# A mixture-of-experts stage: each expert's rows gathered behind its predecessor's down products, and a fifth block of expert 0 loaded ahead

## The chip, the cores and the metric

One Trainium2 chip, one of its cores. The metric is device time in microseconds (us) of one execution. The kernel before has a median of 1833.7 us over 3 runs (1831.3 to 1837.27).

## The reference, cut to what matters

The program computes three blocks of a network one after the other (256 tokens, 1024 channels, all in f32). The change lies in the second half of the first block, an expert-choice layer of 16 experts, each of which takes the 32 tokens that rate it highest:

```python
def _expert_choice_ffn(h, w_router, b_router, w_gate, w_up, w_down):
    b, n, d = h.shape
    cap = max(1, EC_CAPACITY_FACTOR * n // N_EXPERTS)          # 2 * 256 // 16 = 32
    logits = h.astype(jnp.float32) @ w_router.astype(jnp.float32) + b_router.astype(jnp.float32)
    aff = jax.nn.softmax(logits, axis=-1)
    gate, idx = lax.top_k(jnp.swapaxes(aff, 1, 2), cap)
    xs = jax.vmap(lambda hb, ib: hb[ib])(h, idx)
    a = jnp.einsum('becd,edf->becf', xs, w_gate)               # w_gate, w_up: 16 x 1024 x 2048
    u = jnp.einsum('becd,edf->becf', xs, w_up)
    y = jnp.einsum('becf,efd->becd', jax.nn.silu(a) * u, w_down) * gate[..., None].astype(h.dtype)
    return jax.vmap(lambda yb, ib: jnp.zeros((n, d), yb.dtype).at[ib.reshape(-1)].add(yb.reshape(-1, d)))(y, idx)
```

The weights of one expert are 3 matrices of 1024 x 2048 f32 (25.2 MB together), of all sixteen 402.7 MB. The rest of the program (a mixer before, two more blocks behind) is not touched.

## The kernel before, in words

All weights come through a **ring** of 4 slots in SBUF. A slot holds one block of 2 MB (128 partitions x 4096 f32). SyncE (SP) issues the loads in program order, all on one queue; before the load of a block it waits until TensorE has used the block four places earlier (semaphore `ring_used`, one step for each block used up). The layers ahead of the experts use 21 blocks (`EXP_BLOCK0`), then come the experts, then `dense2`.

An expert has 12 blocks: 0 to 3 gate, 4 to 7 up, 8 to 11 down. For a gate or up block TensorE runs 32 matmuls (stationary: 32 columns of `XSE`, the expert's 32 rows turned so that channels lie on partitions; moving: 512 columns of the weights), into bank 0 for gate and bank 1 for up. ScalarE takes silu of bank 0, VectorE multiplies with bank 1 (`HID`), TensorE turns it, ScalarE copies it out (`HIDT`), and then come the products with the down blocks into banks 2 and 3 (in the code `c` = 0 to 3 is down block 8 + c). ScalarE and VectorE each copy one of these banks to `YE`. Last, eight matmuls (`SELT`, a 32 x 256 matrix that places the rows at their tokens and weights them; in the trace they are line L2077, "the combine" below) add the expert's rows to banks 4 to 7, where the sum over all experts grows. Only then do the gate products of the next expert start, on `XSE` of that expert. Experts 1 to 14 are one loop body on every engine; 0 and 15 are written out.

**Where the rows come from.** A gather is a matmul with a matrix of zeros and ones, `SEL` (token x slot, 16 x 32 slots): for each of 8 channel tiles 4 matmuls (2 halves of the tokens, times a high and a low part of the values, `HT_HIGH` and `HT`). For expert 0 this is done first, with 32 columns of `SEL`, 32 matmuls in all (the function `gather`), and VectorE writes `XSE` from the banks with scale and shift (L2675). For the other 15 experts it is done once, behind the down products of expert 0: `gather_rest` runs 32 matmuls with 480 columns each, into banks 0 and 1 in turn; ScalarE (`tokens_in`) writes each of the 8 results with scale and shift into a table `XS` (17 tiles of SBUF, 1 KB a partition each); and VectorE copies 256 columns of it to `XSE` for each next expert (`next_rows`, L2695).

**Blocks loaded ahead.** Of expert 0 the blocks in `EXTRA` (2, 4, 5 and 6) don't go through the ring, but into SBUF that is free at that time (`AHEAD`: two halves of 1 MB each). SP issues them behind the first four blocks of expert 0 that do use the ring (0, 1, 3 and 7), in front of the remaining ones, and TensorE waits for them by `extra_in`. The next ring block of expert 0, block 8, is loaded in two halves: the first when the first half of block 0's slot has been read (`half_read`), the second when all of it has.

```python
            in_ring = [b for b in range(EXP_BLOCKS) if b not in EXTRA]
            for b in in_ring[:RING]:
                load(first_expert_block(b), expert_source(0, b).unsqueeze(1))
            sp.wait_ge(s.ring_used, EXP_BLOCK0)
            for b, halves in zip(EXTRA, AHEAD):
                ...
                    sp.dma_start(halves[kk], ...).then_inc(s.extra_in, 16)
            for b in in_ring[RING:]:
                ...
```

Line numbers of the trace: L1516, L1559 and L1561 are ring loads of SP outside loops, L1554 the loads ahead, L1570 the loop of experts 1 to 15, L1575 `dense2`; L1644 is the helper behind most matmuls, L2057 the turning of `HID`, L2077 the combine, L2121 the helper behind all of ScalarE's activations, L2705 VectorE's copy to `YE`, L2702 `SELT`.

## Time and profile before

| | before |
|---|---|
| median of 3 runs | 1833.7 us (1831.3 to 1837.27) |
| the profiled execution | 1832.58 us |
| its span | 1830.8 us |
| busy: TensorE / its weight loads | 1462.0 us (80%) / 990.6 us (54%) |
| busy: VectorE, ScalarE, GpSimd | 710.5 us (39%), 589.2 us (32%), 35.6 us (2%) |
| moved by DMA | 573.55 MB, mean 313 GB/s |
| mean granted TensorE clock | 0.897 |

The span begins with the first instruction and ends with the last; 1.8 us of the execution lie outside it. The page shows the span in 40 slices of 45.8 us, each with the busy tenths of the engines, the granted clock and what the DMA engines moved. The experts' products stand from 230 us to 1145 us, slices 6 to 25. In the chain of waits a step is either an engine's work or "DMA x<-y", time in which the end of a transfer was waited for.

### The profile page before, as it was taken

What the parts mean: (1) busy time and instruction counts of PE and PEld (TensorE: products, weight loads), DVE (VectorE), ACT (ScalarE), POOL (GpSimd) and SP (SyncE); (2) the same over time, 40 slices, a digit from 0 to 9 for tenths busy, and PEclk for the clock granted to TensorE, in tenths of its full rate; (3) what the DMA queues carried; (4) which work ended last, traced back from release to release, by engine and by line L of the source; (5) the groups of instructions that cost most, each with busy time, mean ns of one, the idle gap of its engine ahead of it and who ended that gap; (6) DMA issues with size and microseconds to landing.
All of it is one profiled execution on the core that took longest, in us unless ns stands there. A gap on an engine that the chain in (4) does not pass through costs nothing.

```text
span 1830.8 us, 25067 instructions
## 1 busy us (share of the span) xinstructions
PE 1462.0 (80%) x10432; PEld 990.6 (54%) x10432; DVE 710.5 (39%) x1256; ACT 589.2 (32%) x1007; POOL 35.6 (2%) x40
## 2 busy tenths in 40 slices
PE   6999996665656666666656667999999999999998
PEld 4787941211112111112111112998998999999997
DVE  4457610000000000000000000897995999478764
ACT  6444510000000000000000001677475776465654
POOL 0000200000000000000000000000000000000101
PEclk9999897888887787877878877999999999999999
DMA  9566799999999999999999999657453755554330
GB/s 399 221 246 235 301 386 424 428 428 429 429 429 428 428 429 428 429 428 428 428 429 429 429 428 427 242 188 207 154 185 132 267 206 190 191 173 173 139 139 24
DMA packets 53266, 573.55 MB, mean 313 GB/s; under 512 B 4928, under 2 KB 15424, under 8 KB 16576
## 3 DMA queue, kind: packets, MB, share of 16 engines
q1 hardware_dynamic: 47440, 563.10, 75.7%
q10 hardware_dynamic: 5744, 9.28, 1.4%
q8 instruction: 61, 1.00, 0.2%
q14 instruction: 21, 0.17, 0.0%
HBM read 568.04 MB, written 4.33 MB: 313 GB/s over the span
## 4 chain that ended last, share of the span: by engine, by line
DMA 43%; PE 37%; DVE 16%; ACT 2%; issue 1%; SPq 0%; DVEq 0%; ACTq 0%
PE bank L1644 36%; DMA ring<-in_w_up 14%; DMA ring<-in_w_down 14%; DMA ring<-in_w_gate 13%; DVE ring_rounded L2437 6%; DVE work L929 2%; DVE work L747 1%; DMA ring<-in_dense 1%; DVE work L919 1%; DVE work_rounded L2360 1%; DMA work<-decay_rows 1%; ACT work L2121 1%; DVE work L738 1%; ACT weights_high_rounded L2121 1%; DMA ring<-in_w_ada 1%
## 5 line engine op out<-in xcount | busy, mean ns | idle before, releaser
L1644 PE MATMUL bank<-ring,work 128*32 128x512 f32 x3008 | 483.9, 778 | 293.5 <-DMA ring<-in_w_up 126.3
L1644 PEld LDWEIGHTS bank<-ring,work 128*32 128x32 f32 x3008 | 94.1, 127 | 646.8 <-DMA ring<-in_w_up 206.6
L2121 ACT ACTIVATE work<-bank 128x512 f32<-128x512 f32 (+3 forms) x152 | 72.8, 492 | 998.6 <-PE bank L1644 667.9
L2437 DVE TENSOR_TENSOR ring_rounded<-ring,weights_high_rounded 128x1024 fp32r<-128x1024 f32 x208 | 252.6, 1219 | 80.9 <-ACT weights_high_rounded L2121 80.9
L2121 ACT ACTIVATE weights_high_rounded<-ring 128x1024 fp32r<-128x1024 f32 x244 | 254.0, 1051 | 42.7 <-PE bank L1644 41.4
L2691 DVE TENSOR_TENSOR work<-work,bank 128x512 f32<-128x512 f32 x16 | 16.5, 1030 | 582.7 <-PE bank L1644 582.7
L1644 PE MATMUL bank<-h_high_rounded,weights_high_rounded 128*128 128x256 f32 x1264 | 185.5, 286 | 1.7 <-ACT h_high_rounded L2121 1.5
L1644 PE MATMUL bank<-h_high_rounded,ring_rounded 128*128 128x256 f32 x1264 | 174.5, 277 | 2.4 <-DVE ring_rounded L2448 2.4
L1644 PE MATMUL bank<-h_normed_rounded,weights_high_rounded 128*128 128x256 f32 x1264 | 173.7, 278 | 0.0
L1644 PEld LDWEIGHTS bank<-h_high_rounded,weights_high_rounded 128*128 128x128 f32 x1264 | 161.3, 188 | 13.2 <-issue 6.9
L1644 PEld LDWEIGHTS bank<-h_high_rounded,ring_rounded 128*128 128x128 f32 x1264 | 158.3, 188 | 2.9 <-DVE ring_rounded L2448 2.8
L1644 PEld LDWEIGHTS bank<-h_normed_rounded,weights_high_rounded 128*128 128x128 f32 x1264 | 157.9, 188 | 0.2
L1644 PE MATMUL bank<-work_rounded,weights_high_rounded 128*128 128x256 f32 x1152 | 152.1, 283 | 5.3 <-ACT work_rounded L2121 5.3
L1644 PEld LDWEIGHTS bank<-work_rounded,weights_high_rounded 128*128 128x128 f32 x1152 | 141.9, 192 | 9.4 <-ACT work_rounded L2121 6.9
L2705 DVE COPY work<-bank 128x512 f32<-128x512 f32 x16 | 11.1, 692 | 284.0 <-PE bank L1644 284.0
L2077 PE MATMUL bank<-work 128*128 128x256 f32 x256 | 70.1, 434 | 13.5 <-DVE work L2705 13.5
L2077 PEld LDWEIGHTS bank<-work 128*128 128x128 f32 x256 | 55.0, 221 | 44.2 <-issue 35.1
L1644 PE MATMUL bank<-work_rounded,ring_rounded 128*128 128x256 f32 x544 | 74.5, 280 | 0.0
L1644 PEld LDWEIGHTS bank<-work_rounded,ring_rounded 128*128 128x128 f32 x544 | 68.3, 191 | 0.0
L1627 POOL TENSOR_TENSOR squares<-squares 128x256 f32<-128x256 f32 x30 | 30.1, 1005 | 1770.8 <-ACT squares L2121 1770.8
L2448 DVE TENSOR_TENSOR ring_rounded<-ring,weights_high_rounded 128x1024 fp32r<-128x1024 f32 x36 | 43.6, 1221 | 44.1 <-ACT weights_high_rounded L2121 43.8
L2121 ACT ACTIVATE work<-work,params 128x256 f32<-128x256 f32 x85 | 48.5, 581 | 27.3 <-DVE work L738 17.8
(269 smaller groups left out, 1206.4 us busy)
## 6 DMA issues: line engine op xcount, KB each, us to landing
ring<-in_w_gate SPq DMA_DIRECT2D x63, 2048.0 KB, 16.2
ring<-in_w_down SPq DMA_DIRECT2D x63, 2048.0 KB, 16.2
ring<-in_w_up SPq DMA_DIRECT2D x61, 2048.0 KB, 16.3
ring<-in_dense SPq DMA_DIRECT2D x60, 2048.0 KB, 8.4
ring<-in_w_ada SPq DMA_DIRECT2D x12, 2048.0 KB, 13.5
work<-in_w_up SPq DMA_DIRECT2D x3, 1024.0 KB, 14.6
bias_diagonals<-work SPq DMA_DIRECT2D x2, 1536.0 KB, 14.9
ring<-in_dense SPq DMA_DIRECT2D x2, 1024.0 KB, 18.7
```

Of the source, the lines that this page charges most:

```text
L738: v.tensor_tensor(dst, B[(PU2 + u) % 4][:, 0:SEQ], RS[:, 1, :], ALU.mult).then_inc(s.dense_sb, 1)
L747: v.scalar_tensor_tensor(out=o[:, shift:SEQ], in0=SCALED2[:, u % 4, 0:SEQ - shift], scalar=w[:, 3 - shift:4 - shift], in1=o[:, shift:SEQ], ...
L919: v.tensor_tensor(SCALED[:, u % 4, :], B[(PU2 + L_UP + u) % 4][:, 0:SEQ], RS[:, 1, :], ALU.mult).then_inc(s.dense_sb, 1)
L929: v.scalar_tensor_tensor(out=o[:, shift:SEQ], in0=SCALED[:, u % 4, 0:SEQ - shift], scalar=ffn_weight(u, 2 - shift), in1=o[:, shift:SEQ], o ...
L1627: nc.gpsimd.tensor_tensor(SQ[:, 0, :], SQ[:, 0, :], SQ[:, k, :], ALU.add).then_inc(s.squares_added, 1)
L1644: return nc.tensor.matmul(o, lhsT, rhs, start=start, stop=stop)
L2077: last = nc.tensor.matmul(B[4 + k // 2][:, (k % 2) * SEQ:(k % 2 + 1) * SEQ], YE[:, k * P:(k + 1) * P], SELT[:], start=False, stop=final an ...
L2121: return nc.scalar.activation(o, i, f, **kw)
L2360: v.tensor_tensor(as_r(full), full, as_r(high) if high.dtype == F32 else high, ALU.subtract).then_inc(s.act_low, 1)
L2437: v.tensor_tensor(as_r(w), w, w_high[:, buffer, :], ALU.subtract).then_inc(s.w_low, 1)
L2448: v.tensor_tensor(as_r(w), w, w_high[:, unit % HIGHS, :], ALU.subtract).then_inc(s.w_low, 1)
L2691: v.tensor_tensor(HID.rearrange("p (i q) -> p q i", i=4), rows_apart(SG), rows_apart(B[1][:]), ALU.mult).then_inc(s.hid_ready, 1)
```

## The change

- `EXTRA` has a fifth block, 8 (the first down block of expert 0), and `AHEAD` a fifth place, tiles 8 to 23 of the work area, which held part of the table `XS`. TensorE waits for it by a semaphore of its own, `down_in`. Block 9 is now the one loaded in two halves. All later blocks stand one place earlier in the ring (`EXP_BASE` is 16, was 17).
- `XS`, `gather_rest`, ScalarE's `tokens_in`, VectorE's `next_rows` and a memset of 0.27 us are gone.
- Behind the down products of each expert but the last, and in front of its combine, TensorE runs `gather_next(e)`: 32 matmuls with 32 columns of `SEL` each, all into bank 1, which are picked by a register in the loop. VectorE, behind its copy to `YE`, waits for them and writes `XSE` in 8 operations out of bank 1, as it does for expert 0.

```diff
-EXTRA = (2, 4, 5, 6)
+EXTRA = (2, 4, 5, 6, 8)
 EXP_BASE = EXP_BLOCK0 - len(EXTRA)
...
-        XS = tiles(8, 17).rearrange("p (k j) -> p k j", k=KT)
...
-                 (h_high, tiles(29, 8)), (squares, h_normed))
+                 (h_high, tiles(29, 8)), (squares, h_normed), (tiles(8, 8), tiles(16, 8)))
...
-                    sp.dma_start(halves[kk], expert_source(0, b)[:, kk * DEXP:(kk + 1) * DEXP]).then_inc(s.extra_in, 16)
+                    sp.dma_start(halves[kk], expert_source(0, b)[:, kk * DEXP:(kk + 1) * DEXP]).then_inc(
+                        s.extra_in if b < 8 else s.down_in, 16)
...
-            def gather_rest():
-
-                pe.wait_ge(s.sel_ready, 2)
+            def gather_next(e):
+
                 for k in range(KT):
-                    if k >= 2:
-                        pe.wait_ge(s.xs_sb, k - 1)
-                    gather(k, B[k % 2][:, CAP:], slice(CAP, EXPERTS * CAP))
-                pe.wait_ge(s.slots_ready, 1)
-                clear(2)
-                clear(3)
+                    for part in (HT_HIGH, HT):
+                        for t in range(TT):
+                            last = mm(B[1][:, k * CAP:(k + 1) * CAP], as_r(part[:, t, k * P:(k + 1) * P]),
+                                      as_r(SEL[:, t, bass.ds(e * CAP + CAP, CAP)]), part is HT_HIGH and t == 0,
+                                      part is HT and t == TT - 1)
+                last.then_inc(s.xs_mm, 1)
...
-                    last.then_inc(s.ring_used, 1)
+                    if not (first and 8 + c in EXTRA):
+                        last.then_inc(s.ring_used, 1)
 
                 if first:
-                    gather_rest()
+                    pe.wait_ge(s.sel_ready, 2)
+                if not final:
+                    gather_next(e)
+                if first:
+                    pe.wait_ge(s.slots_ready, 1)
+                    clear(2)
+                    clear(3)
                 pe.wait_ge(s.selt_ready, e + 1)
...
-            def tokens_in():
-
-                for k in range(KT):
-                    act.wait_ge(s.xs_mm, KT + k + 1)
-                    fn(XS[:, k, CAP:EXPERTS * CAP], B[k % 2][:, CAP:], ACT.Identity, scale=ROW_SCALE[:, k:k + 1],
-                       bias=ROW_SHIFT[:, k:k + 1]).then_inc(s.xs_sb, 1)
...
-            v.memset(XS[:, :, EXPERTS * CAP:], 0.0)
...
-                def next_rows():
-                    v.tensor_copy(XSE, XS[:, :, bass.ds(e * CAP + CAP, CAP)]).then_inc(s.xse_ready, 1)
-
                 if first:
                     other_slots()
-                else:
-                    next_rows()
...
                 v.tensor_copy(YE[:, 512:1024], B[3][:]).then_inc(s.y_high, 1)
-                if first:
-                    dve.wait_ge(s.xs_sb, KT)
-                    next_rows()
+                if final:
+                    return
+                dve.wait_ge(s.xs_mm, e + (KT + 1))
+                for k in range(KT):
+                    last = v.tensor_scalar(XSE[:, k, :], B[1][:, k * CAP:(k + 1) * CAP], ROW_SCALE[:, k:k + 1],
+                                           ROW_SHIFT[:, k:k + 1], ALU.mult, ALU.add)
+                last.then_inc(s.xse_ready, 1)
```

How the instructions stand now. First SP, before and with the change, from the last loads ahead to the loop of the experts (`squares`, `h_normed` and `work` are places of loads ahead; `in_w_down` is the source of blocks 8 to 11). Before:

```order
L1554 DMA squares<-in_w_up 128x2048
L1554 DMA h_normed<-in_w_up 128x2048
L1559 DMA ring<-in_w_down 128x2048
L1561 DMA ring<-in_w_down 128x2048
L1516 DMA ring<-in_w_down 128x4096 x3
```

With the change:

```order
L1553 DMA squares<-in_w_up 128x2048
L1553 DMA h_normed<-in_w_up 128x2048
L1553 DMA work<-in_w_down 128x2048 x2
L1559 DMA ring<-in_w_down 128x2048
L1561 DMA ring<-in_w_down 128x2048
L1515 DMA ring<-in_w_down 128x4096 x2
```

Two loads of 1 MB, block 8, stand in front of the load that waits for `half_read`; three ring blocks follow (9 in halves, 10, 11) where there were four.

Second TensorE in the loop of experts 1 to 14, from the turning of `HID` (L2057, now L2059) to the end of the body. Before:

```order
L2057 MATMUL bank<-consts,work 128x128 x4
L1644 MATMUL bank<-ring,work 32x512 x24
L2034 REGISTER_ALU
L1644 MATMUL bank<-ring,work 32x512 x8
L2077 MATMUL bank<-work 128x256 x8
L2085 REGISTER_ALU
L2085 COMPARE_AND_BRANCH
```

With the change:

```order
L2059 MATMUL bank<-consts,work 128x128 x4
L2036 REGISTER_ALU
L1644 MATMUL bank<-ring,work 32x512 x32
L1644 ISA
L1644 MATMUL bank<-work_rounded 128x32
L1644 ISA
L1644 MATMUL bank<-work_rounded 128x32 x31
L2086 MATMUL bank<-work 128x256 x8
L2094 REGISTER_ALU
L2094 COMPARE_AND_BRANCH
```

The 32 small matmuls of the gather, with two register instructions, stand between the down products and the combine.

Third VectorE in the same loop. Before:

```order
L2691 TENSOR_TENSOR work<-work,bank 128x128x4
L2695 ISA
L2695 COPY work<-work 128x256
L2702 ISA
L2702 TENSOR_SCALAR work<-consts,small 128x256
L2704 REGISTER_ALU
L2705 COPY work<-bank 128x512
```

With the change:

```order
L2690 TENSOR_TENSOR work<-work,bank 128x128x4
L2695 ISA
L2695 TENSOR_SCALAR work<-consts,small 128x256
L2697 REGISTER_ALU
L2698 COPY work<-bank 128x512
L2701 REGISTER_ALU
L2703 TENSOR_SCALAR work<-bank,small 128x32 x8
```

The copy to `XSE` in the middle of the body is gone, and 8 operations that read bank 1 stand at its end.

## Rows read from the trace of the kernel before

**Rows 1.** The page: DMA's rate in 40 slices; chain of waits by engine

```profile
GB/s 399 221 246 235 301 386 424 428 428 429 429 429 428 428 429 428 429 428 428 428 429 429 429 428 427 242 188 207 154 185 132 267 206 190 191 173 173 139 139 24
...
DMA 43%; PE 37%; DVE 16%; ACT 2%; issue 1%; SPq 0%; DVEq 0%; ACTq 0%
```

**Rows 2.** Windows: us; busy PE, PEld, DVE, ACT, POOL (count); clock, DMA share, GB/s

```profile
205.00:230.50 25.50, 23.02 (x150) 21.88 (x153) 18.75 (x72) 12.01 (x33) 5.24 (x6) 0.78 1.00 410
230.50:236.00 5.50, 5.50 (x44) 1.38 (x40) 0.00 (x0) 0.00 (x0) 0.00 (x0) 0.78 0.52 161
236.00:253.00 17.00, 16.31 (x125) 5.04 (x117) 2.71 (x5) 1.20 (x2) 0.00 (x0) 0.91 1.01 422
253.00:256.00 3.00, 3.00 (x32) 0.99 (x28) 0.00 (x0) 0.00 (x0) 0.00 (x0) 0.94 0.94 360
256.00:273.00 17.00, 17.00 (x88) 10.04 (x84) 0.99 (x2) 6.62 (x9) 0.00 (x0) 1.00 1.00 427
273.00:277.00 4.00, 4.00 (x40) 1.15 (x36) 0.00 (x0) 0.00 (x0) 0.00 (x0) 1.00 0.93 340
...
282.00:1120.00 838.00, 520.55 (x3028) 141.24 (x3024) 30.24 (x56) 25.08 (x42) 0.00 (x0) 0.80 1.01 429
```

**Rows 3.** Timeline, loads issued by SP around the end of the loads ahead

```profile
214.15 0.43 SPq L1554 DMA_DIRECT2D h_normed<-in_w_up  x1
232.27 0.33 SPq L1559 DMA_DIRECT2D ring<-in_w_down  x1
233.54 0.33 SPq L1561 DMA_DIRECT2D ring<-in_w_down  x1
...
252.61 0.35 SPq L1570 DMA_DIRECT2D ring<-in_w_gate  x1
254.86 3.77 SPq L1570 DMA_DIRECT2D ring<-in_w_gate  x3
273.47 3.77 SPq L1570 DMA_DIRECT2D ring<-in_w_up  x3
```

**Rows 4.** Timeline, TensorE from expert 0's down products to expert 1's gate products

```profile
249.33 8.77 PE L1644 MATMUL bank<-ring,work 128*32 128x512 f32 x64 [0.69 <-ACT work L2121]
...
258.03 7.97 PE L1644 MATMUL bank<-work_rounded 128*128 128x480 f32 x32
...
271.49 7.07 PE L1644 MATMUL bank<-ring,work 128*32 128x512 f32 x64
```

**Rows 5.** Timeline and lines: expert 0's gather, VectorE's eight operations, a register-picked operation

```profile
225.83 3.90 PE L1644 MATMUL bank<-work_rounded 128*128 128x32 f32 x32
...
L2675 DVE TENSOR_SCALAR work<-bank,small x8: 309/310/311, 226.7 to 229.8; 128x32 f32<-128x32 f32 x8
...
L2702 DVE TENSOR_SCALAR work<-consts,small x16: 395/400/412, 247.9 to 1122.0; 128x256 f32<-128x256 f32 x16
```

**Rows 6.** Timeline, two of the passages between experts 1 to 15; last row a full-clock combine

```profile
555.68 6.10 PE L2077 MATMUL bank<-work 128*128 128x256 f32 x16 [0.90 <-DVE work L2705]
563.70 11.02 SPq L1570 DMA_DIRECT2D ring<-in_w_up  x4
575.61 1.92 PE L1644 MATMUL bank<-ring,work 128*32 128x512 f32 x16 [1.27 <-DMA ring<-in_w_up]
...
383.35 13.47 SPq L1570 DMA_DIRECT2D ring<-in_w_up  x4
399.40 2.98 PE L1644 MATMUL bank<-ring,work 128*32 128x512 f32 x16 [2.97 <-DMA ring<-in_w_up]
...
612.70 3.69 PE L2077 MATMUL bank<-work 128*128 128x256 f32 x16 [0.90 <-DVE work L2705]
```

**Rows 7.** Windows: the products of one block at each level of the clock

```profile
551.20:554.70 3.50, 3.50 (x16) 0.53 (x16) 0.00 (x0) 0.00 (x0) 0.00 (x0) 0.50 1.01 431
381.36:384.70 3.34, 1.93 (x17) 0.42 (x16) 0.00 (x0) 0.00 (x0) 0.00 (x0) 1.00 1.04 442
```

**Rows 8.** Timeline, the last down products of expert 15

```profile
1138.43 1.92 PE L1644 MATMUL bank<-ring,work 128*32 128x512 f32 x16 [0.99 <-DMA ring<-in_w_down]
```

More of the change, by code:

```diff
@@ L103 @@
 state_mm score_mm sd_ready y_mm mod_ready start_in toep_mm toep_sb rot_mm state_sb qfb_ready y_sb y_sums
-ysq_ready turn_ready router_mm aff_ready aff_tr topk_ready slot_mm sel_ready xs_sb xs_mm slots_ready
-half_read xse_ready hid_ready hid_tr hidt_sb selt_ready y_low y_high acc_done act_step params_in ctx_in x_in
+ysq_ready turn_ready router_mm aff_ready aff_tr topk_ready slot_mm sel_ready xs_mm slots_ready
+half_read down_in xse_ready hid_ready hid_tr hidt_sb selt_ready y_low y_high acc_done act_step params_in ctx_in x_in
 toep_stored ramp_ready xi_ready g_silu yc_ready yvar_ready yrstd_ready token_squares expert_in
@@ L2025, in expert_block @@
                         if b in EXTRA:
-                            pe.wait_ge(s.extra_in, 32 * len(EXTRA))
+                            if b < 8:
+                                pe.wait_ge(s.extra_in, 32 * sum(extra < 8 for extra in EXTRA))
+                            else:
+                                pe.wait_ge(s.down_in, 32)
                             return AHEAD[EXTRA.index(b)]
                         blk = first_expert_block(b)
-                        if b == 8:
+                        if b == 9:
                             pe.wait_ge(s.first_units, 32)
@@ L2300, in _, with expert @@
             fn(small(120, 2 * KT), B[6][:, CAP:CAP + 2 * KT], ACT.Copy).then_inc(s.ht_sb, 1)
-            def tokens_in():
-                for k in range(KT):
-                    act.wait_ge(s.xs_mm, KT + k + 1)
-                    fn(XS[:, k, CAP:EXPERTS * CAP], B[k % 2][:, CAP:], ACT.Identity, scale=ROW_SCALE[:, k:k + 1],
-                       bias=ROW_SHIFT[:, k:k + 1]).then_inc(s.xs_sb, 1)
-            def expert(e, gates, first=False):
+            def expert(e, gates):
                 act.wait_ge(s.ring_used, e * EXP_BLOCKS + gates)
@@ L2315, in expert @@
                 fn(YE[:, 0:512], B[2][:], ACT.Copy).then_inc(s.y_low, 1)
-                if first:
-                    tokens_in()
-            expert(0, first_expert_block(3) + 1, first=True)
+            expert(0, first_expert_block(3) + 1)
             with act.Fori(1, EXPERTS) as e:
@@ L2685, in other_slots, with expert @@
                 dve.wait_ge(s.slots_ready, 1)
-            def expert(e, first=False):
-                dve.wait_ge(s.ring_used, e * EXP_BLOCKS + (EXP_BASE + 8))
+            def expert(e, products, first=False, final=False):
+                dve.wait_ge(s.ring_used, e * EXP_BLOCKS + products)
                 dve.wait_ge(s.silu_sb, e + 1)
@@ L2705, in expert @@
                 v.tensor_copy(YE[:, 512:1024], B[3][:]).then_inc(s.y_high, 1)
-                if first:
-                    dve.wait_ge(s.xs_sb, KT)
-                    next_rows()
-            expert(0, first=True)
-            with dve.Fori(1, EXPERTS) as e:
-                expert(e)
+                if final:
[5 more added lines that the diff above has]
+                last.then_inc(s.xse_ready, 1)
+            expert(0, first_expert_block(7) + 1, first=True)
+            with dve.Fori(1, EXPERTS - 1) as e:
+                expert(e, EXP_BASE + 8)
+            expert(EXPERTS - 1, EXP_BASE + 8, final=True)
             for q in range(2):
```

## The prediction

> **What bounds the kernel now.** I read the slices of the page first. From the seventh to the twenty-fifth the DMA engines move 424 to 429 GB/s without a let-up; behind that it is 242 and less, but for one slice of 267 [rows 1]. So the experts' stage runs at the pace of the weight stream, whatever TensorE does in its gaps; 43% of the chain of waits is DMA [rows 1]. The windows say it closer: 429 GB/s over 838 us without a break [rows 2]. At that rate a block of 2,097,152 bytes takes 4.89 us. The last down product of expert 15 still waits for its block [rows 8], so whatever the stream gains or loses before 1138 us, the end gains or loses. Nothing behind that point is touched.
>
> The question is therefore: where does the stream lose time, and what does the change do there? The windows answer with length x (1 - rate / 429) [rows 2]:
> - 230.5 to 236 us: 5.5 x (1 - 161/429) = 3.44 us. The loads ahead, the last of them issued at 214.15 us, have all landed. The next load waits for the first half of block 0 to be read and goes out at 232.27, its second half at 233.54 [rows 3].
> - 236 to 253: 17 x 7/429 = 0.28 us.
> - 253 to 256: 3 x 69/429 = 0.48 us.
> - 256 to 273: 0.08 us.
> - 273 to 277: 4 x 89/429 = 0.83 us.
>
> Together 5.1 us. From 282 us on there is nothing to win.
>
> **The price of a late issue.** Both small losses are loads issued too shortly before the queue ran out. Behind 230.5 us four blocks (8 to 11 of expert 0) were moved: 230.5 + 4 x 4.89 + 3.44 + 0.28 = 253.8 us. The next load was issued at 252.61 [rows 3], 1.2 us ahead, and 0.48 us were lost. Four blocks on it is 253.8 + 0.48 + 19.56 + 0.08 = 273.9; the issue at 273.47 is 0.4 us ahead, and 0.83 us were lost. So a load must be issued some 1.5 us before the queue is empty (1.2 + 0.48 = 1.7 and 0.4 + 0.83 = 1.2), and each us less costs about one.
>
> **The change, part by part.**
>
> *The fifth block ahead.* Its two loads stand behind the one of 214.15 us and in front of the wait for half of block 0, with no wait of their own. They are issued by 215.5 us while the queue is full to 230.5. The stream goes on to 235.4, and block 9 comes at 232.27, 3 us ahead. The loss of 3.44 us is gone: **-3.44**. Nothing ahead of it in the queue is delayed, and SP has nothing to issue between 214.6 and 232.3. On the ring the load of expert 1's block 0 now follows the up products of block 7. Its block 1 follows block 9's down product, as before: 254.86 us [rows 3].
>
> *The next two edges.* The queue now holds blocks 8 to 11 and expert 1's block 0: 230.5 + 5 x 4.89 + 0.28 = 255.2 us. The issue at 254.86 is 0.4 us ahead, which by the same pair costs 0.83 us (it was 0.48). Then 255.2 + 0.83 + 3 x 4.89 + 0.08 = 270.8 us. Block 4 of expert 1 needs block 0 used. TensorE ends the down products at 258.03 and then ran 32 gather matmuls of 480 columns in 7.97 us [rows 4]. With 32 columns the same count took 3.90 us [rows 5]. Clears and combine follow, 266.0 to 271.49, 5.5 us, and block 0's products, 1.98 us up to the issue at 273.47 [rows 3, 4]: 258.03 + 3.90 + 5.5 + 1.98 = 269.4, 1.4 us ahead. I charge 0.48 for it, the nearer of the two prices (it was 0.83). Together 1.31 against 1.31: **0**. Eight activations of ScalarE and the memset leave too; the activations went with the matmuls that are gone, the memset lay beside products.
>
> *The 14 other passages.* Each gets 32 matmuls of 32 columns on TensorE in front of the combine: 3.90 us. TensorE stood idle 0.9 us there anyway for the copies to `YE` [rows 6], so the gate products come 3.0 us later. VectorE's eight operations take 8 x 0.31 = 2.5 us [rows 5] and run beside the combine of 3.69 us [rows 6]; they end about a us before it. The one thing queued behind is the next load. How late may it be? In the tightest of the 14 passages the load of block 4 was issued at 563.70 and used at 575.61 [rows 6]: 11.9 less 4.89 for itself and 1.5 for the lead leaves **5.5 us** of slack. In the loosest, 383.35 to 399.40 [rows 6], it is 9.7, and the mean of the 14 is 7.8. The delay of 3.0 fits in all: **0** in the time, some 55 us more TensorE work. If the cover went, each passage would cost up to 3 us. Unknown is what a register in the operand costs a matmul. On VectorE the nearest case costs nothing: `SELT` takes 395 to 412 ns, once written out and 15 times with a register [rows 5]. I take 0. The upper end is the 480-column matmul, 249 ns each, so 8.0 us a gather and a delay of 7.1. That loses 1.6 us in each of the two tightest passages and about 1.7 in the three next, 5 us in all.
>
> **Sum:** 1832.58 (the profiled execution, 1830.8 of it span) - 3.44 = 1829.1 us. The median of the runs lies 1.1 us above that execution, so I forecast **1830.3 us**, 0.19% less.
>
> The lead is where a page and the rows differ. The Trainium skill, DMA: Bandwidth & Descriptors, section Anatomy of one DMA, gives a transfer a fixed cost of about 2.0 us. If all of it had to be in front, as an estimate the two edges would lose 1.6 and 0.6 us, and the time would be 0.9 us higher than mine. The rows show 1.2 and 1.7, and I go by them.
>
> **The rivals.**
> - *The gap only moves.* The stream is half a us short at 255 us already. If the products of blocks 8 and 9 both run at half clock (a block takes 3.5 us at 0.50 and 1.93 at 1.00 [rows 7]), they end at 256.3, 1.1 us behind the empty queue, and the loss there is 2.6 us, 1.8 more than I charge. A slow gather, combine and gate product could cost another 1 to 2 us at 271. That gives all 3.4 back: about 1834 us. For it: the clock is 0.78 and 0.91 in the windows before [rows 2]. Against it: four down blocks took 8.77 us in this trace [rows 4], one slow block and three fast. Chance 0.12.
> - *Every gather at half clock.* The mean clock of the stage is 0.80 [rows 2]. A gather then takes 3.90 x 3.5/1.93 = 7.1 us, the delay is 6.2, and only the three passages with slack of 5.5, 5.5 and 6.05 lose, 1.6 us together: 1832 us. Against it: 9 of 14 combines ran in 3.69 us, at full clock, and the gather adds work there. Chance 0.08. The Trainium skill, TensorE: Matmul & The Clock Gate, section HAM oscillation, describes just such short bursts between DMA waits as falling back to 1.2 GHz; by that page this case would be the normal one; here the blocks' products ran at both levels [rows 7], and most combines at the upper one.
> - *Slower: the passages become the bound.* If a gather with register operands takes 9 us (280 ns a matmul, more than twice the row), gate products come 8.1 us late, over the mean slack of 7.8. The fourteen lose about 10 us together: 1830.3 + 10 = 1840 us. At 10 us it would be 20. Below about 7 us nothing happens, and a net loss begins at 8 us. For it: no row shows TensorE with such an operand. Against: VectorE's. Chance 0.09.
> - *The change doesn't do what it says.* The fifth block could be held until the gap is over; its loads have no wait and stand first in line, so only something unseen in the queue could. 1833.7 us, chance 0.03.
>
> **How the numbers follow.** The forecast has 0.68. A measurement of this kernel can tell about 0.3% (5.5 us) from no change. Even all 5.1 us regained would be 0.28%, so "faster" needs the scatter of the runs, which is -2.4 to +3.6 us about the median: 0.15. "Slower" is the third rival and a little of the first: 0.11. The rest, 0.74, is "same". The range: below, the 4.7 us that could be regained at best (all but the 0.36 lost at running pace) and most of the scatter, 1826.5; above, the first two rivals with scatter, 1837. The third rival and the far tails stay out.
>
> **What would show it.** Right: the window from 230.5 to 236 at 429 GB/s; one small dip at 254 to 257 us and at most one at 270 to 272; from there 429 GB/s to the end; the last product of expert 15 at about 1135.0 instead of 1138.43; 32 matmuls of 122 ns between down products and combine, and the combine 3 us later against its last down product. Wrong: dips in the rate between 300 and 1120 us (third rival, or the second if the clock is at 0.50 where they stand), a gap of over 2 us near 255 or 271 (the first), or no idle gap gone at 231 (the fourth).

## The result, and the profile after

The changed kernel takes 1836.9 us (median of 22 runs, 1830.9 to 1843.7) against 1833.7 (22 runs of the kernel before beside them): a ratio of 1.0019, 95% interval 1.001 to 1.0028. It is slower by about the amount that I had forecast as a gain; the interval lies just above 1. The profiled execution took 1835.9 us, 1834.1 of it span, 3.3 more than before, at a mean granted clock of 0.887 (0.897 before).

The page of the changed kernel: busy time of the engines, DMA's rate in 40 slices, the chain of waits by engine, and the combine's group.

```profile
PE 1526.5 (83%) x10880; PEld 1072.1 (58%) x10880; DVE 734.7 (40%) x1359; ACT 583.3 (32%) x999; POOL 35.6 (2%) x40
...
GB/s 400 223 243 239 301 383 426 414 428 429 428 428 428 423 430 428 429 428 424 430 428 429 428 425 424 252 187 197 150 192 138 261 204 193 193 173 172 139 138 24
...
PE 40%; DMA 39%; DVE 16%; ACT 3%; issue 1%; SPq 0%; DVEq 0%; ACTq 0%
...
L2086 PE MATMUL bank<-work 128*128 128x256 f32 x256 | 92.7, 541 | 0.9 <-DVE work L2698 0.9
```

TensorE is busy for 65 us more (1462.0 before). The combine, whose code did not change, went from 70.1 to 92.7 us: 22.6 of the 65. In the chain TensorE has taken 3 to 4% from DMA.

The stream first. Windows of the changed kernel, columns as in [rows 2]:

```profile
230.50:236.00 5.50, 5.50 (x28) 1.28 (x32) 0.00 (x0) 0.00 (x0) 0.00 (x0) 0.53 1.01 420
236.00:253.00 17.00, 16.31 (x125) 5.34 (x121) 2.70 (x5) 1.19 (x2) 0.00 (x0) 0.89 1.02 432
253.00:256.00 3.00, 3.00 (x20) 0.79 (x16) 0.00 (x0) 0.00 (x0) 0.00 (x0) 0.50 0.68 284
256.00:269.00 13.00, 13.00 (x87) 7.60 (x80) 2.53 (x9) 0.60 (x1) 0.00 (x0) 0.89 0.83 337
273.00:277.00 4.00, 4.00 (x44) 1.21 (x40) 0.00 (x0) 0.00 (x0) 0.00 (x0) 1.00 0.77 283
282.00:1120.00 838.00, 582.95 (x3460) 221.84 (x3452) 53.19 (x154) 25.08 (x42) 0.00 (x0) 0.78 1.00 427
```

The gap at 231 is closed: 420 GB/s where [rows 2] have 161. But 253 to 256 went from 360 to 284, behind it stands 337 for 13 us where 427 stood, and 273 to 277 went from 340 to 283. From 282 us on the rate is 427 instead of 429. Added up over windows of one us, as us x (1 - rate / 429):

| stretch, us | 230 to 245 | 245 to 262 | 262 to 282 | 282 to 1138 |
|---|---|---|---|---|
| before | 3.8 | 0.5 | 0.8 | 1.1 |
| after | 0.1 | 3.9 | 1.3 | 4.2 |

The 1.1 of the last column is what rounding of the rates leaves where nothing is lost; kernels below that lose nothing there have 0.8 to 1.3. Up to 282 us the changed kernel loses 5.3 us and the one before 5.1: the gap has only moved. Behind it, it loses 3.1 more. Together 3.3, and that is the difference of the spans: what stands ahead of the stretches and behind the last product of expert 15 agrees within 0.2 us in these two traces (692.4 and 692.6 us behind it). It does not in all the traces below.

The same stretch in the timeline of the changed kernel, SP's issues and TensorE between expert 0's down products and expert 1's gate products:

```profile
214.48 0.93 SPq L1553 DMA_DIRECT2D work<-in_w_down  x2
232.42 0.33 SPq L1559 DMA_DIRECT2D ring<-in_w_down  x1
...
251.32 3.64 PE L1644 MATMUL bank<-work 128*32 128x512 f32 x16 [0.69 <-ACT work L2130]
257.52 0.34 SPq L1570 DMA_DIRECT2D ring<-in_w_gate  x1
260.68 3.75 PE L1644 MATMUL bank<-work_rounded 128*128 128x32 f32 x32
266.26 5.41 PE L2086 MATMUL bank<-work 128*128 128x256 f32 x16
271.60 7.07 PE L1644 MATMUL bank<-ring,work 128*32 128x512 f32 x64
273.58 5.48 SPq L1570 DMA_DIRECT2D ring<-in_w_up  x4
```

And the combine of expert 0 in the kernel before:

```profile
267.84 3.72 PE L2077 MATMUL bank<-work 128*128 128x256 f32 x16
```

The two loads of block 8 (214.48) went out as forecast. The down products began at 251.32, 2.0 us later than in [rows 4], and block 8's ran at half clock in 3.64 us. So expert 1's block 1 was issued at 257.52 instead of 254.86, behind a queue that was empty at about 255.3. The gather, the clears and the combine then ended at 271.60 us, as late as before (271.49), although the matmuls of 480 columns are gone, and block 4 was issued at 273.58 (273.47 in [rows 3]).

Two of the fourteen passages, in the timeline of the changed kernel: gather, combine, VectorE's eight operations, the next load.

```profile
325.74 6.39 PE L2086 MATMUL bank<-work 128*128 128x256 f32 x16
325.94 1.84 DVE L2703 TENSOR_SCALAR work<-bank,small 128x32 f32<-128x32 f32 x8 [6.24 <-PE bank L1644]
334.05 5.48 SPq L1570 DMA_DIRECT2D ring<-in_w_up  x4
...
494.85 3.75 PE L1644 MATMUL bank<-work_rounded 128*128 x32
498.44 5.38 PE L2086 MATMUL bank<-work 128*128 128x256 f32 x16
498.63 1.84 DVE L2703 TENSOR_SCALAR work<-bank,small 128x32 f32<-128x32 f32 x8 [2.96 <-PE bank L1644]
```

And windows: the gather and the start of the combine behind it in the second of these, and a gather at half clock in the thirteenth passage.

```profile
494.85:498.44 3.59, 3.59 (x36) 3.59 (x33) 0.69 (x1) 0.60 (x1) 0.00 (x0) 1.00 1.00 424
498.44:500.20 1.76, 1.76 (x6) 1.49 (x6) 1.57 (x8) 0.00 (x0) 0.00 (x0) 0.51 1.00 428
1084.24:1091.09 6.85, 6.85 (x37) 6.85 (x33) 0.69 (x1) 0.60 (x1) 0.00 (x0) 0.50 1.00 426
```

In the first row the gather runs at a clock of 1.00 (2.4 GHz), 3.59 us, with no idle time; in the second the combine begins at 0.51 (1.2 GHz). Not one of the 14 combines took 3.69 us, which 9 did before; they took 5.03 to 6.63. Four gathers (318.89, 613.45, 848.34 and 1084.24 us) ran at half clock as a whole, in 6.85 us: there the clock was low already when the gather began, behind a last down product that was partly or wholly at half clock, and the gather did not bring it back. Those four passages are the ones that lose: from one expert's first up products that wait for their block to the next expert's it is 59.9, 59.0, 59.4 and 60.0 us there, where the kernel before has 58.74 (twelve blocks of 4.895). In the other ten it is 58.7 to 58.8.

The last down product of expert 15, for [rows 8]:

```profile
1141.53 1.92 PE L1644 MATMUL bank<-ring,work 128*32 128x512 f32 x16 [1.19 <-DMA ring<-in_w_down]
```

It is 3.1 us later than before. Behind it nothing changed.

### The profile page after: what moved, and what is told of

It reads as the page before. It is cut to its first block, busy times and chain, and to the rows that moved or that the text cites. A ratio compares the mean times of both kernels' runs of the same rounds, so it can differ in the third digit from the quotient of the medians.

```text
span 1834.1 us, 26054 instructions
## 1 busy us (share of the span) xinstructions
PE 1526.5 (83%) x10880; PEld 1072.1 (58%) x10880; DVE 734.7 (40%) x1359; ACT 583.3 (32%) x999; POOL 35.6 (2%) x40
## 4 chain that ended last, share of the span: by engine, by line
PE 40%; DMA 39%; DVE 16%; ACT 3%; issue 1%; SPq 0%; DVEq 0%; ACTq 0%
PE bank L1644 37%; DMA ring<-in_w_up 14%; DMA ring<-in_w_down 14%; DMA ring<-in_w_gate 9%; DVE ring_rounded L2437 6%; DVE work L928 2%; PE bank L2086 2%; DMA ring<-in_w_ada 1%; DVE work L746 1%; DVE work L918 1%; ACT work L2130 1%; DMA work<-decay_rows 1%; DVE work_rounded L2360 1%; DVE work L737 1%; ACT weights_high_rounded L2130 1%
## 5 line engine op out<-in xcount | busy, mean ns | idle before, releaser
L1644 PE MATMUL bank<-ring,work 128*32 128x512 f32 x2992 | 459.9, 752 | 244.8 <-DMA ring<-in_w_up 131.8
L2437 DVE TENSOR_TENSOR ring_rounded<-ring,weights_high_rounded 128x1024 fp32r<-128x1024 f32 x208 | 252.7, 1220 | 79.3 <-ACT weights_high_rounded L2130 79.2
L2086 PE MATMUL bank<-work 128*128 128x256 f32 x256 | 92.7, 541 | 0.9 <-DVE work L2698 0.9
L1644 PEld LDWEIGHTS bank<-work_rounded 128*128 128x128 f32 (+1 forms) x514 | 75.3, 236 | 19.4 <-issue 19.2
L2086 PEld LDWEIGHTS bank<-work 128*128 128x128 f32 x256 | 71.7, 287 | 18.0 <-issue 2.5
L1644 PE MATMUL bank<-work_rounded 128*128 (+2 forms) x514 | 77.4, 299 | 0.0
```

Source lines behind the costliest of these rows:

```text
L1644: return nc.tensor.matmul(o, lhsT, rhs, start=start, stop=stop)
L2086: last = nc.tensor.matmul(B[4 + k // 2][:, (k % 2) * SEQ:(k % 2 + 1) * SEQ], YE[:, k * P:(k + 1) * P], SELT[:], start=False, stop=final an ...
L2437: v.tensor_tensor(as_r(w), w, w_high[:, buffer, :], ALU.subtract).then_inc(s.w_low, 1)
```

## The experiments

Sixteen runs of fourteen kernels, on four chips. Ratios are to the kernel before on the same chip, with their 95% intervals; the profile is of one execution of each, which need not be a typical one. Four numbers in braces, as {3.8, 0.5, 0.8, 1.1}, are a kernel's losses in the four stretches of the table above.

**First question: the two parts, each alone.** `block_only` is the kernel before with block 8 ahead; the table's zeros are written behind the down products.

```diff
-EXTRA = (2, 4, 5, 6)
+EXTRA = (2, 4, 5, 6, 8)
...
-            v.memset(XS[:, :, EXPERTS * CAP:], 0.0)
...
+                    v.memset(XS[:, :, EXPERTS * CAP:], 0.0)
```

> Before, with the fifth block (8) loaded ahead alone; the table XS stays, its memset moves behind the down products. Theory A (both parts cost: the gap at 231 us only moves to 255 us, and the passages lose 3.4 us by the gather): no gap at 231, but one of 1 to 3 us at 255 to 258, so 0 to -2 us against the kernel before; no loss in any passage from 300 us on. Theory B (the block is worth its full 3.4 us, and the gather costs all of 6.6): -3.4 us, that is -0.19%, and hardly a gap at 255.

Measured: 0.9977 (0.9965 to 0.9989), {1.4, 2.4, 3.7, 1.2}. The trace shows no gain at all: 8.7 us are lost against 6.2 (all four stretches added up). Windows of `block_only`:

```profile
256.00:262.00 6.00, 6.00 (x52) 1.61 (x44) 0.00 (x0) 0.00 (x0) 0.00 (x0) 0.86 0.67 251
273.00:277.00 4.00, 4.00 (x26) 2.56 (x28) 0.00 (x0) 0.00 (x0) 0.00 (x0) 1.00 0.52 221
```

The gap stands at 256 and 273 now. That the runs came out 0.23% faster all the same is taken up below.

`gather_only` is the changed kernel with four blocks ahead.

```diff
-EXTRA = (2, 4, 5, 6, 8)
+EXTRA = (2, 4, 5, 6)
```

> After, with only four blocks ahead: the gather behind each expert alone. Theory A: the gap at 231 us is there again, the one at 255 us is small, the passages lose about 3.4 us in the three or four whose gather runs at half clock (6.85 us): about +3 us against the kernel before. Theory B: +6.6 us.

Measured: 1.0018 (1.0004 to 1.0032), {3.4, 1.0, -0.1, 6.1}. As slow as the whole change. The gather costs time, and the fifth block beside it gains nothing.

**Second question: the gather's place.** `gather_split` runs its 32 matmuls as 12, 12 and 8 behind the first three down blocks, where TensorE waits for the next block anyway, and VectorE's eight operations ahead of its copy of the down products.

```diff
+                    if not final and c < 3:
+                        if first and c == 0:
+                            pe.wait_ge(s.sel_ready, 2)
+                        gather_next(e, range(3 * c, min(3 * c + 3, KT)))
...
-                if not final:
-                    gather_next(e)
```

> After, with the 32 matmuls of the gather cut in three (12, 12, 8) and put behind the first, second and third down block, where TensorE waits 2.9 us for the next block; VectorE writes XSE before its copy to YE. Theory A: no passage loses anything (429 GB/s from 300 to 1120 us, passages of 58.74 us), time 3.4 us under the changed kernel, about that of before. If the loss came from something else in the passages (VectorE, registers), it stays.

Measured: 0.9987 (0.9971 to 1.0003), {2.1, 2.3, 0, 1.2}. 11 of 14 combines take 3.69 us again, and no passage loses.

`split_ten` is this with block 10 of expert 0 ahead in block 8's stead, so that SP's next loads hang on other down products.

> The kernel of the last run with block 10 instead of 8 as the fifth one ahead, so that the load of expert 1's block 1 hangs on the first down product of expert 0 and not on the second. Theory A: the gap at 255 us shrinks from 2.5 us to under 1, 2 to 3 us less than with block 8, so 2 to 4 us under the kernel before. Theory B: same as the run before it.

Measured: 0.9984 (0.9966 to 1.0001), {0.2, 0, 1.2, 1.1}. Windows of `split_ten`:

```profile
230.50:236.00 5.50, 5.50 (x40) 2.29 (x43) 0.66 (x3) 0.00 (x0) 0.00 (x0) 0.69 1.01 419
269.00:273.00 4.00, 4.00 (x38) 1.20 (x40) 0.00 (x0) 0.00 (x0) 0.00 (x0) 1.00 0.88 332
282.00:1120.00 838.00, 586.07 (x3476) 204.70 (x3468) 53.15 (x154) 25.07 (x42) 0.00 (x0) 0.79 1.01 428
```

Of all losses one dip of about a us is left; the stage runs at the stream's pace behind it. The same kernel once more:

> The split gather with block 10 ahead once more. Last-edge theory: the edge comes some 2 to 3 us earlier, since no 480-column gather stands there, so 2 to 4 us lost less than before: 0.998 to 0.999, the best kernel that computes the whole.

Measured: 0.9986 (0.9971 to 1.0), {2.0, 0, 1.1, 1.3}. And the split gather with four blocks ahead:

> The split gather with four blocks ahead: the new way of gathering alone, placed in TensorE's waits. Theory A: nothing lost from 300 us on, the gap at 231 us as before: 0 +- 1.5 us against before. If gathering for each expert costs something wherever it stands: +2 us or more.

Measured: 1.0008 (0.9994 to 1.0022), {6.0, 0, 0.1, 1.3}. Part of its 6.0 is that the stream broke at 231 for longer than in the kernel before (40 GB/s in the window there, where [rows 2] have 161). Beside the split gather the fifth block is worth some 0.2%, by kernels on different chips whose intervals overlap a little.

**Third question: what a gather costs on TensorE, on VectorE.** `gather_twice` runs each gather twice.

```diff
-                    gather_next(e)
+                    gather_next(e, False)
+                    gather_next(e)
```

> The changed kernel with every gather run twice (64 small matmuls in each passage). Theory A (TensorE's time in the passage pushes the next load past the slack): the second gather mostly runs at half clock, so the load of block 4 comes 7 to 10 us later than before where 5.5 to 9.7 us can be borne: 2 to 5 us lost in each of 14 passages, 30 to 60 us in all over the changed kernel, dips in the rate at every passage. If TensorE's time there is covered: under 5 us.

Measured: 1.0362 (1.0332 to 1.0392), {1.5, 2.1, 8.3, 59.8}. Windows of `gather_twice`, one passage: its first gather, the second, the combine.

```profile
522.28:525.90 3.62, 3.62 (x36) 3.62 (x32) 0.69 (x1) 0.60 (x1) 0.00 (x0) 0.96 1.01 430
525.90:532.84 6.94, 6.94 (x35) 6.94 (x35) 0.00 (x0) 0.00 (x0) 0.00 (x0) 0.50 0.99 423
532.84:538.18 5.34, 5.34 (x21) 4.20 (x25) 1.84 (x8) 0.00 (x0) 0.00 (x0) 0.69 0.89 377
```

The first gather at full clock takes 3.6 us, 112 ns a matmul, and the very same work behind it 6.9 at half clock; the combine suffers too. Two gathers take 10.1 to 11.0 us (13.7 in one passage where both ran at half clock), and the passages lose 2.3 to 8.4 us each, 4.3 in the mean. This kernel also shows what a load costs when the queue has run empty, in its timeline: the issue of a block 4 and its first product.

```profile
540.10 5.48 SPq L1570 DMA_DIRECT2D ring<-in_w_up  x4
547.29 1.92 PE L1644 MATMUL bank<-ring,work 128*32 128x512 f32 x16 [2.10 <-DMA ring<-in_w_up]
```

That is 7.2 us, and in all its passages it is 7.1 to 7.3, of which the block itself takes 4.89 at the stream's pace.

`vector_twice` doubles VectorE's eight operations, into a tile that nobody reads.

> The changed kernel with VectorE's eight operations on the gathered rows run twice, the first time into a tile that nobody reads: 1.8 us more on VectorE behind each gather. Theory A: still ends before the combine (5.0 us and more), so the same time as the changed kernel, 0 +- 2 us. Rival (XSE comes late and holds the next gate products): about +1.8 us a passage, up to 10 to 25 us in all.

Measured: 0.9994 (0.9978 to 1.0011), {2.6, 2.0, 4.9, 5.7}. The eight took 1.84 us and the doubles 1.83, beside the combine: doubling them cost nothing, so VectorE is not the cause. But the time is no confirmation of the rest: it was forecast within 2 us of the changed kernel (1.0019) and came out 4.6 us under it, while this trace, of an execution of 1838.7 us where the median is 1832.0, loses 15.2 us. That is not explained.

**Fourth question: is it the time on TensorE, or the clock?** Three kernels put work without a purpose in the gather's place of the kernel before: 32 matmuls of 32 columns at fixed addresses (`small_idle`), 28 of 128 columns in plain fp32 (`wide_idle`), and 14 of those (`wide_short`).

```diff
+                elif not final:
+                    for n in range(32):
+                        mm(B[1][:, 0:CAP], as_r(HT[:, n % 2, 0:P]), as_r(SEL[:, n % 2, 0:CAP]))
```

> The kernel before with 32 matmuls of 32 columns in each of the 14 passages, at fixed addresses, whose result nobody reads. Theory A with the clock (narrow matmuls let the granted clock fall though TensorE is busy): hardly a combine at 3.69 us (9 of 14 before), 5.0 to 6.6 instead; +3 to +5 us against before, as the changed kernel. If registers or VectorE's work in the passage were the cause: no loss here.

Measured: 1.0034 (1.002 to 1.0048), {4.7, 1.8, 1.4, 6.5}. None of 14 combines at 3.69 us; they take 5.06 to 6.63, and the filler 3.59 to 6.85. Windows of `small_idle`, filler and combine:

```profile
853.22:856.81 3.59, 3.59 (x36) 3.59 (x33) 0.69 (x1) 0.60 (x1) 0.00 (x0) 1.00 0.99 420
856.81:862.20 5.39, 5.39 (x22) 4.25 (x25) 0.00 (x0) 0.00 (x0) 0.00 (x0) 0.68 1.01 432
```

It is the picture of the changed kernel without registers in the operands, VectorE's operations or a moved load.

> The kernel before with 28 f32 matmuls of 128 x 128 in each of the 14 passages instead (0.128 us each at full clock, 3.6 us, as long as the 32 narrow ones). Clock theory: most combines stay at 3.69 us, nothing is lost after 300 us, 0 +- 2 us against before. If it is only the length of the work: as the run with the narrow ones, +3 to +5 us.

Measured: 1.0004 (0.9993 to 1.0016), {6.2, 0.5, 1.1, 5.1}. Timeline of `wide_idle`, filler and combine of one passage, and below it the windows of both:

```profile
498.36 6.52 PE L1644 MATMUL bank<-ones 128*128 128x128 f32 x56
504.71 3.62 PE L2079 MATMUL bank<-work 128*128 128x256 f32 x16
```

```profile
501.00:504.70 3.70, 3.70 (x35) 3.70 (x34) 0.00 (x0) 0.00 (x0) 0.00 (x0) 1.00 1.01 430
504.70:508.30 3.60, 3.60 (x22) 2.91 (x23) 0.00 (x0) 0.00 (x0) 0.00 (x0) 1.00 1.00 428
```

All 14 combines take 3.62 us at a clock of 1.00, although the filler was longer than meant: each of the 28 is recorded as two passes and takes 0.22 us, about 6.2 in all, where I had reckoned 3.6 from a row of 16 records that are 8 matmuls. That surplus is the likely reason why the fourth stretch still loses. With half as many:

> The kernel before with 14 f32 matmuls of 128 x 128 in each passage, 3.1 us at full clock (28 took 6.2 us, since each is recorded as two passes), so as long as 32 narrow ones at full clock or a little less. Clock theory: all combines at 3.62 to 3.69 us, nothing lost after 300 us, 0 +- 1.5 us against before, where the narrow ones cost +6.4 us. If length is the cause: +3 us or more.

Measured: 1.0006 (0.9993 to 1.0019), {4.2, 0.7, 1.0, 0.8}. 14 of 14 combines at 3.62 us, and no passage loses anything. Five of these fillers began at half clock too, as the four slow gathers did. Windows of `wide_short`, one such filler in two parts and the combine:

```profile
378.61:380.00 1.39, 1.39 (x10) 1.39 (x7) 0.69 (x1) 0.60 (x1) 0.00 (x0) 0.50 1.08 460
380.00:382.73 2.73, 2.73 (x24) 2.73 (x23) 0.00 (x0) 0.00 (x0) 0.00 (x0) 0.91 0.97 414
382.73:386.35 3.62, 3.62 (x22) 2.93 (x24) 0.00 (x0) 0.00 (x0) 0.00 (x0) 1.00 1.01 430
```

The clock rose within the wide work, which took 4.12 us at most; it stayed at 0.50 through 6.85 us of narrow work. So about 3 us of TensorE in front of the combine are free, as the prediction had it; 3.6 us of narrow matmuls are not: the clock falls behind them, and where it is low it does not come back in them.

**Fifth question: what the fifth block is worth.** `block_ten` is `block_only` with block 10, `ten_gather` the changed kernel with block 10.

> The run of the fifth block alone (table kept), with block 10 instead of 8 ahead, so the load of expert 1's block 1 hangs on the first down product. Theory A: no gap at 231 us, under 1 us lost at 255, 1 us at 273, nothing later: -3.5 to -4.7 us against before (0.1974 to 0.26%), the best of the kernels without the split. Rival (block 8's edge cost little on the mean of runs, its trace was one draw of the clock): as block 8 alone, -3 to -4 us.

Measured: 1.0000 (0.9986 to 1.0014), {2.1, 0, 4.7, 1.0}. The forecast of 3.5 to 4.7 us gained missed: the last edge (273 us) is worse than before.

> The changed kernel with block 10 instead of 8 ahead; the gather stays in front of the combine. If block and gather add up: gather alone (+3.3 us) and the block's -3.5 to -4.2, about 0 against before. If the block is worth nothing beside the gather, as block 8 seemed to be (1.0019 with, 1.0018 without): +3 us.

Measured: 1.002 (1.0006 to 1.0034), {0, 0.1, 2.2, 5.2}. The gap at 255 is gone with block 10, and the time is that of the changed kernel. (Its profiled execution, 1830.8 us, was the fastest of the twelve, whose median is 1835.5.)

These suggest that not the first gap decides but the last edge, the issue of expert 1's block 4. To try that, TensorE's way there was shortened: the 32 matmuls of 480 columns and ScalarE's eight writes left out of the kernel before, with four blocks ahead (`free_four`) and with five (`free_five`, block 10). Experts 1 to 15 then work on rows of zeros.

```diff
-                for k in range(KT):
-                    if k >= 2:
-                        pe.wait_ge(s.xs_sb, k - 1)
-                    gather(k, B[k % 2][:, CAP:], slice(CAP, EXPERTS * CAP))
...
-                if first:
-                    tokens_in()
```

> The kernel before without the 32 gather matmuls of 480 columns and ScalarE's eight writes of the table (experts 1 to 15 get no rows of their own; the table is zero), four blocks ahead. Last-edge theory (the loss is the issue of expert 1's block 4, plus 1.5 us, less the end of the loads ahead, less eight blocks of 4.89 us, but no less than what the gap at 231 costs): that issue comes 8 us earlier, the last two dips go, the gap at 231 stays: 4.0 us lost, -1 us against before. First-gap theory: the same, -1 us.

Measured: 0.9985 (0.9973 to 0.9996), {3.5, 0.8, -0.1, 1.2}.

> The same without the big gather, with five blocks ahead (block 10). Last-edge theory: now nothing is late, 0 to 1 us lost before 282 us: 3 to 4 us under the run with four, -4 to -5 us against before (0.9975), where with the gather in place the fifth block gave 1.0000. First-gap theory: the fifth block gives 3.4 us with or without the gather, so 3.4 under the run with four as well, but then block 10 with the table should have shown it too.

Measured: 0.9961 (0.9945 to 0.9976), {0, 0.1, 0, 1.1}. Windows of `free_five`:

```profile
230.50:236.00 5.50, 5.50 (x44) 1.38 (x44) 0.00 (x0) 0.00 (x0) 0.00 (x0) 0.79 1.01 422
253.00:256.00 3.00, 3.00 (x32) 1.00 (x28) 0.00 (x0) 0.00 (x0) 0.00 (x0) 0.94 1.00 421
273.00:277.00 4.00, 1.34 (x16) 0.14 (x5) 0.00 (x0) 0.60 (x1) 0.00 (x0) 1.00 1.02 434
```

No dip is left anywhere, and between the two the fifth block is worth 0.24%, 4.4 us, where the traces differ by 4.1 us of losses: about the whole 3.5 and 0.8 that the one with four loses. The two intervals just touch (0.9973 and 0.9976).

How the loss comes about can be read off SP's issues, here in the timeline of `free_five`: the first loads ahead, the last two (block 10's), and expert 1's block 4.

```profile
204.84 0.91 SPq L1554 DMA_DIRECT2D weights_high<-in_w_gate  x2
205.78 1.01 SPq L1554 DMA_DIRECT2D work<-in_w_up  x2
...
214.66 0.91 SPq L1554 DMA_DIRECT2D work<-in_w_down  x2
...
265.59 9.15 SPq L1571 DMA_DIRECT2D ring<-in_w_up  x4
```

Let S be the issue of the first load ahead (`weights_high`, 204.84 here) and I4 that of block 4 (265.59). In the kernel before, S is 204.79 and its four blocks ahead had landed at 230.5, 25.7 us later. Behind them the stream has eight blocks of 4.89 us to move (expert 0's last four, expert 1's first four) before block 4, and I4 must come 1.5 us ahead of their end. The loss from 230 to 282 us is then I4 + 1.5 - (S + 64.8), however it is spread over the edges before; it can't fall under what those cost by themselves.

| kernel | S | I4 | worked out | measured |
|---|---|---|---|---|
| before | 204.79 | 273.47 | 5.4 | 5.1 |
| after | 204.66 | 273.58 | 5.6 | 5.3 |
| `block_only` | 206.42 | 277.75 | 8.0 | 7.5 |
| `block_ten` | 204.74 | 275.03 | 7.0 | 6.8 |
| `ten_gather` | 205.97 | 272.03 | 2.8 | 2.3 |
| `split_ten` | 206.31 | 271.21 | 1.6 | 1.4 |
| `split_ten_again` | 204.94 | 271.63 | 3.4 | 3.1 |
| `free_five` | 204.84 | 265.59 | none | 0.1 |

Five more traces fit as well, worked out and measured: `block_again` 7.9 and 7.7, `vector_twice` 9.8 and 9.5, `small_idle` 8.2 and 7.9, `wide_idle` 8.1 and 7.8, `wide_short` 6.1 and 5.9. With four blocks ahead the gap at 231 is the floor: `gather_only`, `free_four` and `split_none` could do with 2.7, none and 2.6 by I4, and lose 4.3, 4.2 and 6.1. In `gather_split` the sum gives 3.4 and 4.4 are lost, all at the edges before 262 us. In `gather_twice` I4 lies behind the stretch.

**What stays open.** `block_only` once more:

> The kernel of the first run, block 8 ahead with the table kept, once more. Last-edge theory: the load of expert 1's block 4 still waits for gather_rest, so 0 to -1 us against before (0.9995 to 1.0). If 0.9977 was right: -4 us again.

Measured: 0.9986 (0.9974 to 0.9997), {1.6, 2.1, 4.0, 1.2}. The block beside the table is thus worth -0.23, -0.14 and (block 10) 0.00% in the times, while all three traces lose 7 to 9 us, more than that of the kernel before. One profiled execution a kernel can't settle this. `small_idle`, `wide_idle` and `wide_short` have the instructions of the kernel before up to 282 us, and lose 7.9, 7.8 and 5.9 us there where its own trace loses 5.1; beside those the 7.5, 7.7 and 6.8 of the kernels with the fifth block are nothing unusual. For the same reason 5.3 against 5.1 does not say that block and gather together gain exactly nothing before 282 us. `block_only`'s profiled execution was the slowest of its twelve (1836.6 us, median 1830.3). And two more things move in the spans: the start (S lies between 203.0 and 206.4), and the part behind expert 15's last product, 687.4 to 694.4 us, which no experiment touched. It was 4.5 to 5.0 us shorter in the two traces of the split gather with block 10 than in the kernel before, so their spans of 1824.7 and 1824.8 us are not all the change's doing; why is open.

## Why the prediction was wrong, step by step

Two terms put at nothing failed: the next two edges, where expert 1's block 4 was issued 4.2 us later than the sum had it, so that the 3.44 us were not gained; and the 14 passages, which lost 3.1 us. Both had work at full clock that ran at half.

- **What bounds the kernel** (the stream, read as rate against 429) held. The losses of the two traces add up to the difference of the spans, 3.3 us. The 2.0 us of fixed cost that the prediction cites from the Trainium skill, DMA: Bandwidth & Descriptors, section Anatomy of one DMA, are given there for the path of GpSimd, and SP issues these loads; in the traces the lead of 1.5 us fits the losses within 0.5 us.
- **The fifth block, -3.44.** The step closed the gap at 231 (161 to 420 GB/s) and was still wrong: the stream was not freed by it, since a later edge was due at the same time as before. The 5.1 us before it were never four separate losses; they are what the last edge of the ring left over, and they moved to 255 and 273 (5.3). `free_five` against `free_four` shows about 4.4 us that the block gives where no late edge stands behind it.
- **The next two edges, 0.** Their issues were forecast at 254.86 and 269.4 and came at 257.52 and 273.58. The first moved because the products of expert 0's first blocks (6.20 us where the kernel before took 4.91) and of block 8 (3.64) ran at half clock. In the second, the gather's 3.90 us were right (3.75), but the down products ended at 260.68, 2.65 us later than the sum had them, and the combine took 5.41 where 3.72 stood in the trace of before: 1.69 more. Together they are the 4.2 us by which the issue was late. I had taken each piece at the clock that it had before the change.
- **The 14 passages, 0.** The price of the gather at full clock was right (3.59 us; 3.90 reckoned). The slack was sized too large: 4.89 and 1.5 us were taken off the time from issue to use, while a load into an empty queue takes 7.1 to 7.3 us, which leaves 4.7 us and not 5.5 in the tightest passage and 8.8 in the loosest. What the term lacked was the combine behind it: 3.69 us taken, 5.03 to 6.63 measured. In the four passages whose gather is slow, its 6.85 us less the 0.9 of idle time, 2.2 to 2.7 for the combine and 0.6 to 1.1 for the last down product make a delay of 9.3 us against a passage at full clock. That is over the 8.8, and the four lose 3.3 us together by their lengths (3.1 by the rates). The step "the delay of 3.0 fits in all" failed on the clock; `wide_short` shows that the delay itself fits.
- **Registers in the operand, 0**, held: 112 ns a matmul in the loop, the same as with fixed addresses in `small_idle` (3.59 us for 32). VectorE's eight operations take 1.84 us; 2.5 was reckoned.
- **The rivals.** Two that I gave 0.20 together came true in part, side by side. The gap only moved, at 255 by the slow products that the rival named. Of the gathers 4 of 14 ran at half clock and not all; but they lost 3.1 us, twice what the rival had for all, since it left out the combine. I had said that 9 of 14 combines at full clock spoke against it, and that the gather adds work there. With that work in place none of the 14 ran at full clock. The Trainium skill, TensorE: Matmul & The Clock Gate, section HAM oscillation, has bursts between DMA waits falling back to 1.2 GHz as the normal case; the trace of the kernel before agrees for the last down products, of which 10 of 14 ran partly or wholly at half clock. The page puts the fall down to the waits, and here it also came without one: behind a gather with no idle time.
- **The range** (1826.5 to 1837.0) held the median of 1836.9 by 0.1 us, and only because it was widened for the rivals and the scatter: the forecast had the wrong sign.

The better form of this change is the split gather with block 10 ahead: 0.9984 and 0.9986 against 1.0019 for the kernel as changed. Against the kernel before, both intervals still reach 1 at their upper end.

## What to carry to other kernels

A load ahead is worth only what the last late issue behind it allows: before pricing a gap in a stream, write down for each later edge of the ring when its buffer comes free, and take the largest lateness, not the sum. Work that must go into a serial hand-over should go where the engine waits for data anyway; and where many narrow matmuls stand in front of something that counts, read the granted clock of what follows them, however busy the profile shows TensorE.

## What the runs showed of the hardware

TensorE's clock fell to 0.50 in or behind 32 matmuls of 32 columns though the engine is recorded as busy throughout: behind a gather at 1.00 the combine began at 0.51, and a second gather ran in 6.94 us against 3.62 for the first. With plain fp32 matmuls of 128 columns for 3 or 6 us in the same place the combine ran at 1.00 in 14 of 14 passages. The recorded weight loads do not tell the two apart: they are busy for the whole of the narrow work (3.59 of 3.59 us) and of the wide work (3.70 of 3.70).

The fillers differ from the gather in type and data too (they multiply ones by ones). Type and stationary matrices are the same in expert 0, where the kernel before gathers with 480 columns and the changed one with 32. The combine behind 480 columns took 3.72 us in all seven traces that have them (granted clock 1.00 from 256 to 273 us in [rows 2]); behind 32 columns in one piece it took 5.17 to 5.80 us in five of five. At one type and with the same stationary matrices, then, the 480-column work kept the clock here and the 32-column work did not. The 480-column work also lasts longer (7.97 us against 3.75), and what of the two counts was not separated.

A 2 MB load that SP issued into an empty queue was used 7.1 to 7.3 us later, in all passages of `gather_twice`; at the pace of the running stream a block takes 4.89 us.
